# A product-key expert layer inside a one-core transformer block: the first expert list named on VectorE, with ScalarE's order and one key-score product moved

## The reference

```python
def peer_ffn(x, wq, subkeys, u, v):
    b, s, d = x.shape
    q = (x @ wq).reshape(b, s, PEER_HEADS, 2, PEER_DQ // 2)
    sc = jnp.einsum('bshcd,hckd->bshck', q, subkeys).astype(jnp.float32)
    top_s, top_i = lax.top_k(sc, PEER_TOPK)
    cand = top_s[..., 0, :, None] + top_s[..., 1, None, :]
    cand_i = top_i[..., 0, :, None] * PEER_NKEYS + top_i[..., 1, None, :]
    best_s, best_j = lax.top_k(cand.reshape(b, s, PEER_HEADS, PEER_TOPK * PEER_TOPK), PEER_TOPK)
    expert = jnp.take_along_axis(cand_i.reshape(b, s, PEER_HEADS, PEER_TOPK * PEER_TOPK), best_j, axis=-1)
    g = jax.nn.softmax(best_s, axis=-1)
...
    def tok_fn(args):
        xc, ec, gc = args
        act = jax.nn.gelu(jnp.einsum('td,tkd->tk', xc, u[ec]), approximate=False)
        return jnp.einsum('tk,tkd->td', gc * act, v[ec])
```

## Time and profile before

| what | value |
|---|---|
| median of 3 runs | 1860.69 us (1859.79 to 1861.05) |
| span of the profiled execution | 1855.4 us |
| VectorE busy | 1446.5 us, 78% |
| TensorE busy | 1318.8 us, 71% |
| POOL busy | 798.9 us, 43% |
| ScalarE busy | 769.2 us, 41% |
| mean DMA rate | 311 GB/s |
| VectorE's row products (L1506) | 232 in the trace, 2280 ns each |

### The profile page before, as it was taken

The page is one execution under the profiler, slowest core; times in us unless marked ns, Lnnn a source line. Parts: engine busy times, 40 slices in busy tenths (PEclk is TensorE's granted clock), DMA queues, the critical chain, the costliest instruction groups (busy, mean ns, idle before and its releaser), DMA issues. The chain is left out here.

```text
span 1855.4 us, 24088 instructions
## 1 busy us (share of the span) xinstructions
PE 1318.8 (71%) x7651; PEld 1160.7 (63%) x7651; DVE 1446.5 (78%) x1962; ACT 769.2 (41%) x1349; POOL 798.9 (43%) x854
## 2 busy tenths in 40 slices
PE   7999999999995552000111122289999999999997
PEld 6999999988974430000111111278888888888886
DVE  5334555574368888999999999989999999999855
ACT  4323445554210113000556666673333333333644
POOL 1100000000154444555555555288777777777303
PEclk9999999999997776555555555599999999999999
DMA  7974444456599999999999999919999999999953
GB/s 248 292 221 135 136 137 135 139 202 232 175 374 411 411 415 368 381 397 410 415 404 411 409 414 401 421 58 360 373 363 366 367 360 364 369 364 365 344 184 111
DMA packets 172276, 577.15 MB, mean 311 GB/s; under 512 B 14804, under 2 KB 88869, under 8 KB 138288
## 3 DMA queue, kind: packets, MB, share of 16 engines
q0 software_dynamic: 58544, 367.16, 50.1%
q1 hardware_dynamic: 113664, 209.10, 32.8%
HBM read 571.99 MB, written 7.36 MB: 312 GB/s over the span
## 5 line engine op out<-in xcount | busy, mean ns | idle before, releaser
L1506 DVE SCALAR_TENSOR_TENSOR rows<-rows,banks 128x2048 f32<-128x2048 f32 x232 | 520.2, 2280 | 29.8 <-DMA rows<-peer_u_dram,expert 29.6
L707 POOL DMA_INDIRECT rows<-peer_u_dram,expert x232 | 220.4, 950 | 263.0 <-DVE rows L1506 173.9
L753 POOL DMA_INDIRECT vrow<-peer_v_dram,vidx x224 | 282.0, 1259 | 113.7 <-DVE hres L1584 63.1
L2023 PE MATMUL banks<-hot,hot 128*128 128x128 f32 x512 | 104.0, 371 | 237.1 <-ACT hot L1091 233.3
L2023 PEld LDWEIGHTS banks<-hot,hot 128*128 128x128 f32 x512 | 90.3, 267 | 251.1 <-issue 178.6
L807 ACT CAST whi<-raw 128x2048 fp32r<-128x2048 f32 x80 | 152.2, 1904 | 174.8 <-PE banks L1763 96.9
L1584 DVE SCALAR_TENSOR_TENSOR hres<-vrow,slot_coef,hres 128x704 f32<-128x704 f32 x224 | 213.3, 952 | 3.1 <-DMA vrow<-peer_v_dram,vidx 2.9
L2067 PE MATMUL banks<-vlo,chi 128*128 128x192 f32 x762 | 191.9, 387 | 0.9 <-DVE vlo L1598 0.9
L1598 DVE TENSOR_TENSOR vlo<-vraw,vhi 128x1216 fp32r<-128x1216 f32 x128 | 181.5, 1418 | 0.1
L1271 DVE TENSOR_TENSOR wlo<-raw,whi 128x2048 fp32r<-128x2048 f32 x46 | 106.0, 2305 | 92.6 <-ACT whi L807 91.4
L1134 ACT CAST chi<-spread 128x256 fp32r (+1 forms) x128 | 52.0, 406 | 296.9 <-PE banks L2067 291.2
(11 more groups left out here) (278 smaller groups left out, 2975.0 us busy)
## 6 DMA issues: line engine op xcount, KB each, us to landing
vraw<-peer_v_dram SPq DMA_DIRECT2D x128, 672.0 KB
raw<-w_in_dram SPq DMA_DIRECT2D x48, 1024.0 KB, 5.4
raw<-w_out_dram SPq DMA_DIRECT2D x16, 1024.0 KB, 5.4
wqraw<-peer_wq_dram SPq DMA_DIRECT2D x32, 512.0 KB, 8.8
raw<-ple_gate_dram SPq DMA_DIRECT2D x16, 1024.0 KB, 5.6
rows<-peer_u_dram,expert POOLq DMA_INDIRECT x232
vrow<-peer_v_dram,vidx POOLq DMA_INDIRECT x224
bias_by_distance<-bias_of_heads POOLq DMA_DIRECT2D x1, 3072.0 KB, 12.6
```

What stands on the lines that cost most here:

```text
L707: pool.indirect_dma_start(dst[:, :], None, peer_u[0], bass.IndirectOffsetOnAxis(ap=expert[b][:, k:k + 1], axis=0))\
L753: pool.indirect_dma_start(vrow[j][:, :], None, pieces, bass.IndirectOffsetOnAxis(ap=idx[:, j % TT, j // TT:j // TT + 1], axis=0))\
L1506: dve.scalar_tensor_tensor(out=r[:, :], in0=r[:, :], scalar=1.0, in1=xps[tt][:, :], op0=ALU.mult, op1=ALU.mult, accum_out=dots[b][:, k:k + ...
L2023: last = pe.matmul(bank[SPREAD_BANK[m]][:, a * P:(a + 1) * P], hot2[tt][m][:, a, :], hot1[tt][m][:, a, :], start=True, stop=True)
```

## The change

Four edits. The first step's expert numbers are worked out on VectorE, and POOL only waits for them (`routed`); VectorE also writes the lists that the value gathers use later (`slot_idx`, `slot_row`) for that step. The key scores of head 0 are made behind the first of the four k-blocks in head 1's first piece, and `s1` for step 0 is written straight from PSUM. On ScalarE the gelu of step 2 (`gelu(1, 0)`) stands ahead of `take_head(7)`; the exponentials of step 4 and the scores of step 5 (`route_exp(2, 0)`, `step_scores(5)`) stand ahead of the `p` copies, and the gelu of step 3 (`gelu(1, 1)`) directly behind them, ahead of `copy_x(1)` and `pp_keep`.

```diff
@@ POOL
-            unpack(0)
-            look_up()
-            name_experts(0, 0)
+            pool.wait_ge(routed, 1)
             pool.wait_ge(mm_done["out"], 2 * NG["out"])
             fetch(0, True, ring=early_rows)
@@ ScalarE
-            take_head(0)
-            act.wait_ge(sc_sb, TT)
-            step_scores(0, True)
+            take_queries(0)
+            act.wait_ge(sc_mm, 1)
+            act.activation(s1[:, :, :], bank[2][:, 0:2 * NKEYS].rearrange("p (c k) -> p c k", c=2),
+                           ACT.Copy, scale=rstd[:, 0:1]).then_inc(s1_ready, 1)
+            take_scores(0)
             copy_first_x()
...
             route_exp(1, 1, False)
-            step_scores(4, False)
+            step_scores(4)
+            gelu(1, 0)
             take_head(7)
-            gelu(1, 0)
+            route_exp(2, 0, False)
+            act.wait_ge(sc_sb, TT * PEER_H)
+            step_scores(5)
...
+            gelu(1, 1)
             act.wait_ge(pp_sb, 8)
-            act.wait_ge(sc_sb, TT * PEER_H)
             act.wait_ge(norm_done["ffn"], 1 + 4 * TT)
             copy_x(1)
             act.wait_ge(x_copied, TT)
             for tt in range(TT):
                 act.copy(pp_keep[:, tt, :], pp_made[:, tt, :]).then_inc(pp_sb, 1)
-            route_exp(2, 0, False)
-            step_scores(5, False)
-            gelu(1, 1)
@@ VectorE
+            def name_first_experts():
+
+                dve.wait_ge(chosen, 2)
+                dve.tensor_copy(topf[:, :, :], topi[:, :, :]).then_inc(unpacked, 1)
+                dve.tensor_copy(bidxf[:, :, :], bidx[:, :, :]).then_inc(unpacked, 1)
+                dve.wait_ge(unpacked, 2)
+                st.did(dve.tensor_tensor(pick[:, :, :, :], bidxf[:, :, :, None].broadcast_to([P, 2, TOPK, TOPK]),
+                                         iota[:, None, None, 0:TOPK].broadcast_to([P, 2, TOPK, TOPK]), ALU.is_equal))
+                st.wait()
+                st.did(dve.tensor_tensor(pick[:, :, :, :], pick[:, :, :, :],
+                                         topf[:, :, None, :].broadcast_to([P, 2, TOPK, TOPK]), ALU.mult))
+                st.wait()
+                st.did(dve.tensor_reduce(picked[:, :, :], pick[:, :, :, :], AX.X, ALU.add))
+                st.wait()
+                st.did(dve.scalar_tensor_tensor(out=bidxf[:, 1, :], in0=picked[:, 0, :], scalar=float(NKEYS),
+                                                in1=picked[:, 1, :], op0=ALU.mult, op1=ALU.add))
+                st.wait()
+                dve.tensor_copy(expert[0][:, :], bidxf[:, 1, :]).then_inc(routed, 1)
+                st.did(dve.tensor_copy(slot_idx[:, :, 0:TOPK], picked[:, :, :]))
+                st.did(dve.tensor_scalar(row4[:, :], bidxf[:, 1, :], float(D // PIECE), None, ALU.mult))
+                st.wait()
+                st.did(dve.tensor_copy(slot_row[:, 0:TOPK], row4[:, :]))
+                st.wait()
+                dve.wait_ge(routed, 1)
...
             split_pairs(0)
+            name_first_experts()
             dve.wait_ge(x_copied, 1)
@@ TensorE
                     for k in range(WQ_K):
+                        if g == 1 and r == 0 and k == 1:
+                            key_scores(0)
...
-                    if r == 0 and g >= 1:
+                    if r == 0 and g >= 2:
                         key_scores(g - 1)
```

More of the change, by code:

```diff
@@ L997, in route_exp, with step_scores @@
                     .then_inc(gate_exp, 1)
-            def step_scores(s, peeled):
-                if not peeled:
-                    act.wait_ge(s1_read, 4 * s)
+            def step_scores(s):
+                act.wait_ge(s1_read, 4 * s)
                 act.copy(s1[:, :, :], scores[:, bass.ds(s, 1), :, :].rearrange("p o c k -> p (o c) k"))\
@@ L1032, in _ @@
             act.wait_ge(sc_sb, 2 * TT)
-            step_scores(1, False)
+            step_scores(1)
             take_head(2)
             route_exp(0, 1, False)
-            step_scores(2, False)
+            step_scores(2)
             take_head(3)
@@ L1040, in _ @@
             route_exp(1, 0, False)
-            step_scores(3, False)
+            step_scores(3)
             take_head(5)
@@ L1098, in peer @@
                     if not last:
-                        step_scores(2 * i + b + 2, False)
+                        step_scores(2 * i + b + 2)
                     if spreading:
```

## The result

The changed kernel takes **1846.35 us** (median of 4 runs, 1844.21 to 1847.68), beside 1860.31 us for the kernel before: ratio 0.9927, 95% interval 0.9916 to 0.9939. Forecast were 1855.2 us and a range from 1850.0 to 1860.5. The sign was right, the size was not: 14 us gained where 5.5 were forecast. On a second chip the same program gave 1847.52 against 1859.54 us (6 and 11 runs; ratio 0.9936, 0.9924 to 0.9949). The profiled execution took 1844.21 us, with a span of 1842.2, so the span is 13.2 us shorter. (Around the span lie 2.0 us; the 5.3 that I took for the kernel before came from setting its profile beside the median of other runs.

What follows compares the result with a forecast made beforehand. VectorE's steps, with its waits between 480 and 760 us and the DMA engines full beside the gathers, were taken to set the end. +3.8 - 4.96 - 4.42 = -5.6 us gave 1855.2 us, range 1850 to 1860.5.

Steps and rivals of the forecast that it cites:

- Part 1, step 0: Step 0's start: first gather at 504.9 us, 9.2 us sooner (8 to 10.5); VectorE's first row at about 511.3.
- D: Query weights beside the gathers: pieces from 17 on and heads from head 4 on 16.5 us later; bounds 13 and 20.
- Part 2, ScalarE's order: VectorE's stalls of 4.96 us (gelu behind head 7) and 4.42 us (step 5's scores) both go.
- The gelu behind the `p` copies: Step 3's gelu: might come at 723.8 where VectorE wants it at 721.9; 1.9 us lost, counted only in the range.
- What is late next: Step 4's scores come at 666.8 us; VectorE stands 13 us and goes on 3.8 us later than before.
- the step-2 stall: VectorE in step 2: perhaps 1 to 3 us for step 1's gelu behind `take_head(5)`, made up again before step 3.
- the formula 22.1 - D: End of the steps: the gain is 22.1 us less the heads' delay, and no more than the earlier rows allow.
- the weights are held back less: Rival: heads not late; 9.3 us sooner at step 4 plus 4.4, 13.7 us, 1847; both faster rivals share 0.15.
- The sum itself: End of the steps: +3.8 for step 4's scores, -4.96 and -4.42 for the two late stalls, -5.6 us in all.

Runs made afterwards that it cites:

- early gelu: Changed kernel with the gelu of step 1 ahead of head 5's queries and scores on ScalarE: 1857.49 us, ratio 0.9989 to the kernel before.
- without early scores: Changed kernel without the earlier key scores of head 0, new ScalarE order and VectorE naming kept: 1850.88 us, ratio 0.9949 to the kernel before.
- deeper ring: Changed kernel with pieces 5 to 8 of the query weights loaded into idle gather buffers: 1846.32 us, ratio 0.9924 to the kernel before.
- Naming alone: Kernel before with only step 0's naming moved to VectorE, no early key scores, old ScalarE order: 1869.57 us, ratio 1.0048.
- both together: Changed kernel with four more weight pieces in gather buffers and key scores of heads 3 to 6 ahead of the next head's first piece: 1842.08 us.

## Why the prediction was right in sign and wrong in size

**Part 1, step 0: right.** Every number of it within 0.7 us: `s1` (494.88 against 494.2), the choice, the naming (501.32 to 504.55 with the lists for the value gathers, the 3.2 us forecast), the first gather, the first row. The queries come at 492.58, 0.6 later than before, and so does all that precedes them (VectorE's `rstd` runs at 480.56 instead of 479.99), in code that the change leaves alone.

**D, the delay of the heads: mis-sized.** The step that says "piece 15 is asked for when piece 7 is done, at 507.1, and lands at 518.5". It was asked for at 507.4, but landed near 524 (piece 17 ran at 545.71; two pieces of 10.65 less). The weights' queue moved **no packet at all** from 507 to 511 us, while the gathers moved 172; the DMA queues of that stretch:

```profile
q0 software_dynamic: 172, 1.28, 90.5%
```

and nothing for q1. Nor is that the usual delay of a request: in the kernel before, with no gather running, a piece asked for at 499.7 us had its first packets by 501. So D was 22.4 by my count (22.1 at piece 24), above my upper bound of 20. Taken alone this error would have made the forecast worse: 22.1 - 22.4 is no gain at all. It is not what made the change faster than forecast.

**Part 2, ScalarE's order: right.** Both stalls went, and alone it gave 8.4 us by the ratio where the sum had 9.38. The gelu behind the `p` copies ran at 700.75, not at up to 723.8, and cost nothing.

**"What is late next": here the prediction fails.** The step that failed has step 4's scores at 650.27 + 16.5 = 666.8, VectorE standing 13 us for them and going on 3.8 us later than before. It rests on "all heads from head 4 on" being D late, that is on 10.7 us a piece up to the last one. The runs showed piece 28, behind which head 6's key scores are made, following pieces 26 and 27 with no wait: step 4's scores were there at 659.1, VectorE stood 1.0 us and went on at 659.21, 3.8 us *sooner* than before. With that one term the prediction's own sum is -3.8 - 4.96 - 4.42 = -13.2 us, and the spans differ by 13.2.

I had the step-2 stall as "perhaps 1 to 3 us, made up again before step 3", and the real one behind step 3's first row. With D at 22 the gelu behind head 5 came 8.5 us late, in step 2. It came *instead of* the later stall, as the early gelu shows: the gathers ran thin at 640 us with five pieces of weights left, which took the free turns, and heads 6 and 7 came in time. With the early gelu the 18.77 us stall appears where I had it. In the three kernels that have part 2 and the stall in step 3, the formula 22.1 - D holds within 0.5 us of the spans: -0.1 against 0.4 (early gelu, D of 22.2), 6.8 against 7.1 (without early scores, 15.3), 11.9 against 12.1 (deeper ring, 10.2). Against the medians and ratios it is some 2 to 3 us too low, about what the profiled execution of the kernel before was below its median. So the formula was right wherever its stall was there; in the changed kernel the stall was not.

**The rival "the weights are held back less", 1847: its time was hit by luck, and its reason in part.** Its sum was 9.3 us sooner at step 4 plus 4.4; measured were 3.8 sooner at step 4 plus both stalls, 9.4. "When the eight buffers are full, no gather asks for the engines" was set aside with "the even 10.7 us, which did not change where VectorE was busy". But those rows held no stall long enough to stop POOL: a stall of 8.5 us does, by way of the choice that POOL waits for, and it shows 15 us later. What was wrong in the rival is D: it did not stay small but grew to 22.4 and then went away.

**The sum itself.** (A slip: 1860.69 less 5.6 is 1855.1, not 1855.2.) It priced each stall of VectorE at its length. For the two late stalls that came out; for a stall in step 2, which the sum did not have, it would not. The ledger prices a stall at what the DMA engines fail to move. From 515 to 720 us the changed kernel's engines were never short, with 8.5 us of stall in it; the kernel before was short from 680 to 760 us (383, 372 and 359 GB/s), at and behind its two late stalls, and at 500 to 515, before its gathers (141 against 280). At 411 GB/s, some 5 us of the gain come from 500 to 515 us and 8 to 9 from 680 to 760 us.

## What to carry to other kernels

- Where two queues share full DMA engines, count bytes beside the waits: the time of the stretch is the bytes to move over the full rate, plus what the engines fall short of. Here a stall of the consumer of 8.5 us, while the other queue still had work, left the engines full; one of the same length near the end of that work left them short.
- A queue held back at an even pace need not stay so: ask what happens to it when its rival pauses, and let the forecast have that case. The even 10.6 us a piece ended with one pause of the gathers.
- A start that is earlier for one queue is a delay for another when they take turns by packets; here the one with short runs lost. Naming alone made this kernel 9 us slower. Ask for the short-run data before the long-run data begin, or take what depends on it out of the way (both together: 1842 us).
- Removing a visible wait can lose time (the early gelu, 11 us): it made room for a wait of 18.8 us later on. Before doing so, look which wait it was keeping away.

## What the runs showed of the hardware that I had not expected

- The first piece of weights asked for behind the gathers' start (at 507.4 us) had no packet until 511, where without gathers the first packets came within 1.3 us (asked for at 499.7, kernel before); then one for one with the gathers' (254 beside 255 in 515 to 520 us). Why it starts so late stays open. SyncE's instruction that asks for a piece lasted about 0.4 us up to 518 us, 8.4 us at 522 us and up to 22.5 us later on.
- A piece's time beside the gathers follows its run length: 10.6 us at 1 KB, 20.1 us at 512 bytes, for the same 512 KB; when the gathers were thin the same queue moved 149 GB/s (640 to 650 us).
- A stall of one length had a different worth by its place: with 8.5 us in step 2 (the change) the engines stayed at 411 GB/s, with 8.5 us in step 3 (deeper ring) they were 84 GB/s short over 20 us, 4 us of work. Without that stall the deeper ring took 2.8 us less by the ratios. That the one in step 2 cost nothing is by the ledger; no run takes it away and leaves the rest.
